# DeltaNet recurrence of a two-layer hybrid trunk: one projection step per recurrence step, split by tokens

## The reference, cut to what matters

```python
def step(state, inp):                      # scan over 8 chunks of 64 tokens, 8 heads, 64 x 64 states
    q_i, k_i, u_i, w_i, a_i, g_i = inp
    v_new = u_i - einsum('bhck,bhkv->bhcv', w_i, state)
    o = (einsum('bhck,bhkv->bhcv', q_i * exp(g_i)[..., None], state)
         + einsum('bhcs,bhsv->bhcv', a_i, v_new))
    g_last = g_i[..., -1]
    state = (state * exp(g_last)[..., None, None]
             + einsum('bhck,bhcv->bhkv', k_i * exp(g_last[..., None] - g_i)[..., None], v_new))
    return state, o
...
proj = h @ w_in[l]                         # a_v is 512 columns of this product
y_a = spatial_gating_branch(a_u, a_v, ...)
```

## Time and profile before

| what | us |
|---|---|
| median of 3 runs | 1763.38 (1763.12 to 1763.38) |
| the profiled execution | 1764.11 |
| its span on the core | 1762.3 |
| PE busy | 1744.1 (99%) |
| PE weight loads busy | 1426.3 (81%) |
| VectorE busy | 958.8 (54%) |
| POOL busy | 1066.3 (61%) |
| ScalarE busy | 689.9 (39%) |

### The profile page before, as it was taken

One profiled execution on the slowest core, in us unless ns is written; L12 is line 12 of the kernel. 1 busy time (PEld: TensorE's weight loads), 2 busy tenths in 40 slices (PEclk: granted clock), 3 DMA queues, 4 the chain that ended last, 5 costly groups with the idle time before them and its releaser, 6 DMA issues.

```text
span 1762.3 us, 26300 instructions
## 1 busy us (share of the span) xinstructions
PE 1744.1 (99%) x10006; PEld 1426.3 (81%) x10006; DVE 958.8 (54%) x1565; ACT 689.9 (39%) x1241; POOL 1066.3 (61%) x572
## 2 busy tenths in 40 slices
PE   8999999999999999999999999999999999999999
PEld 7778888778888888888787788887788888888887
DVE  6786636653542455444576866266443435444445
ACT  6433316650104444444355243075411054444442
POOL 6444367235665777777774434662456657777776
PEclk9999999999999999999999999999999999999999
DMA  6222133123235666666542222331332356666655
GB/s 201 85 69 77 49 96 108 37 96 96 84 97 169 157 172 161 161 174 157 130 156 78 71 70 61 96 96 37 108 96 85 97 158 163 159 173 158 169 154 144
DMA packets 58897, 207.18 MB, mean 118 GB/s; under 512 B 6369, under 2 KB 8705, under 8 KB 58785
## 3 DMA queue, kind: packets, MB, share of 16 engines
q1 hardware_dynamic: 47520, 164.94, 29.9%
q0 software_dynamic: 9216, 33.56, 10.2%
q10 hardware_dynamic: 2048, 7.10, 1.1%
HBM read 184.61 MB, written 4.19 MB: 107 GB/s over the span
## 4 chain that ended last, share of the span: by engine, by line
PE 95%; ACT 2%; DVE 2%; issue 1%; DMA 0%; SPq 0%; DVEq 0%; ACTq 0%
PE ps L662 22%; PE ps L664 22%; PE ps L663 22%; PE ps L1259 6%; PE ps L1261 6%; PE ps L1260 6%; PE ps L1131 2%; PE ps L1140 1%; PE ps L1153 1%; PE ps L681 1%; PE ps L904 1%; PE ps L891 0%; DMA xin<-x 0%; PE ps L941 0%; PE ps L1203 0%
## 5 line engine op out<-in xcount | busy, mean ns | idle before, releaser
L662 PE MATMUL ps<-hHi,wHi 128*128 128x512 f32 x1360 | 553.2, 407 | 1.3 <-DVE convd L1916 1.3
L664 PE MATMUL ps<-hHi,wLo 128*128 128x512 f32 x1360 | 530.4, 390 | 0.0
L663 PE MATMUL ps<-hLo,wHi 128*128 128x512 f32 x1360 | 529.8, 390 | 0.0
L562 POOL TENSOR_SCALAR wHi<-wraw 128x1024 fp32r<-128x1024 f32 x168 | 181.4, 1080 | 497.3 <-PE ps L664 480.2
L567 POOL TENSOR_TENSOR wLo<-wraw,wHi 128x1024 fp32r<-128x1024 f32 x168 | 415.2, 2472 | 13.9
L593 POOL TENSOR_TENSOR wLo<-w,wHi 128x1024 fp32r<-128x1024 f32 x96 | 239.2, 2514 | 138.6 <-ACT wHi L1690 138.0
L662 PEld LDWEIGHTS ps<-hHi,wHi 128*128 128x128 f32 x1360 | 255.4, 188 | 61.5 <-issue 6.9
L663 PEld LDWEIGHTS ps<-hLo,wHi 128*128 128x128 f32 x1360 | 255.7, 188 | 54.7 <-issue 3.8
L664 PEld LDWEIGHTS ps<-hHi,wLo 128*128 128x128 f32 x1360 | 255.3, 188 | 54.2
L1259 PE MATMUL ps<-wHi,fHi 128*128 128x512 f32 x448 | 174.8, 390 | 1.8 <-issue 1.8
L1260 PE MATMUL ps<-wLo,fHi 128*128 128x512 f32 x448 | 174.3, 389 | 0.0
(11 more groups left out here) (334 smaller groups left out, 2675.0 us busy)
## 6 DMA issues: line engine op xcount, KB each, us to landing
wraw<-stream SPq DMA_DIRECT2D x224, 512.0 KB, 3.6
w<-stream SPq DMA_DIRECT2D x64, 512.0 KB, 4.4
w<-w POOLq DMA_DIRECT2D x32, 512.0 KB, 6.9
b<-stream SPq DMA_DIRECT2D x16, 512.0 KB, 3.5
b<-stream POOLq DMA_DIRECT2D x16, 512.0 KB, 6.4
w<-stream POOLq DMA_DIRECT2D x16, 512.0 KB, 8.1
xin<-x SPq DMA_DIRECT2D x4, 512.0 KB, 6.8
y<-x ACTq DMA_DIRECT2D x1, 2048.0 KB, 9.9
```

The source lines that it names most:

```text
L562: nc.gpsimd.tensor_scalar(wHi[:, slot], wraw[:, slot % RAW], 1.0, 0.0, ALU.mult, ALU.add).then_inc(unit_high, 1)
L662: mm(o, lh[lc], rh[rc], start=start, stop=False)
L663: mm(o, lh[lc], rl[rc], start=False, stop=False)
L664: return mm(o, ll[lc], rh[rc], start=False, stop=stop)
```

## The change

The block of the projection is cut by tokens. `project_half(tile, k, 0)` does the three products on tokens 0 to 255 and stands where the whole block stood. `project_half(tile, k, 1)` does them on tokens 256 to 511 and stands after the queries of line 916, ahead of the wait for `vnew`. Six matmuls of 128x256 take the place of three of 128x512 in each of the steps 0 to 7. Both halves write one bank; only the first matmul of the first half opens the sum.

```diff
+                def project_half(tile, k, half):
+
+                    n, u = TILE_NO[tile], UNIT_NO[tile]
+                    if k == 0 and half == 0:
+                        pe.wait_ge(bank_read[n % 2], layer * per.bank_read + n // 2)
+                        pe.wait_ge(unit_split, layer * per.unit_split + u + 1)
+                    o = tile_bank(layer, n)[:, half * 256:(half + 1) * 256]
+                    weights, tokens = np.s_[:, u % RING, k * P:(k + 1) * P], np.s_[:, k, half * 256:(half + 1) * 256]
+                    mm(o, wHi[weights], hHi[tokens], start=k == 0 and half == 0, stop=False, skip_group_check=True)
+                    mm(o, wHi[weights], hLo[tokens], start=False, stop=False, skip_group_check=True)
+                    last = mm(o, wLo[weights], hHi[tokens], start=False, stop=k == KD - 1, skip_group_check=True)
+                    if k == KD - 1 and half:
+                        last.then_inc(unit_done, 1)
+
...
                         if step < CHUNKS:
-                            project(("av", 1), range(step, step + 1))
+                            project_half(("av", 1), step, 0)
                         else:
                             turn_delta_output(0)
...
                     if step == 0:
-                        project(("av", 1), range(0, 1))
+                        project_half(("av", 1), 0, 0)
...
                     if step:
                         last.then_inc(query_done, 1)
+                    if step < CHUNKS:
+                        project_half(("av", 1), step, 1)
                     for half in range(2):
                         pe.wait_ge(vnew_done, layer * per.vnew_done + 2 * step + half + 1)
```

## The result

| | median us | lowest to highest |
|---|---|---|
| before | 1763.38 | 1763.12 to 1764.77 |
| after | 1773.30 | 1772.60 to 1773.81 |

The ratio is 1.0054, with a 95% interval of 1.0038 to 1.0070: slower by 9.9 us, where 8.9 were forecast. The profiled execution took 1773.27 us against 1764.11, its span 1771.4 against 1762.3, so +9.1.

What follows compares the result with a forecast made beforehand. PE was taken to bound the kernel, busy 99% and 95% of the chain. Steps 1 to 7 add 4.43 us per layer, twice 8.9, moving the median 1763.38 to 1772.3; range 1770.5 to 1774.5, 8 in 10 1768.0 to 1776.0.

Steps and rivals of the forecast that it cites:

- The first place gives nothing back in steps 2 to 7: Ahead of line 904: block 0.32 us shorter, but line 904's second half still waits for r; gain at most 0.02, counted 0.
- The second half block is paid in full: Between lines 916 and 927, where no wait hides it: +0.72 us in even steps, +0.67 in odd ones.
- the change of tile size: Between 64x64 and full-size matmuls: 0.20 us going in against 0.05, 0.10 coming out; without this drain +5.4 instead of +8.9.
- Step 1: Recurrence step 1: r doesn't hold line 904, so 0.32 us is gained before the added half block; net +0.34, bounds 0.3 and 0.65.
- Step 6: Recurrence step 6: VectorE also scales an output chunk; its 0.08 us extra goes with line 927 later, leaving +0.64.
- Step 0: Recurrence step 0: both half blocks in succession, line 927 possible at 168.26 but waiting for vnew until 168.36; counted 0.
- Seven steps, two layers: Sum over steps 1 to 7: 4.43 us per layer, twice is 8.9.
- A: Rival: PE's own order holds line 904's second half, so steps 2 to 7 gain 0.32 us each; 1768.5, chance 0.08.
- B: Rival: short streams don't hide their weight loads, so a 128x256 matmul costs 0.23 us; +15.3, 1778.7, chance 0.07.
- C: Rival: at least 0.7 us idle ahead of line 927 holds the half block; seven steps lose 0.32 each, 1758.9, chance 0.04.
- D: Rival: PE waits behind the recurrence, for weights or POOL, shorten; between 0 and +3.5 us, say 1765, chance 0.04.
- Both it and PE move by the same amount, so its distance to PE stays: POOL's ring refill after the tile is done: POOL already waits 21.0 us, so the later tile adds no term.

## Why the prediction was right, and where it was not

- *The first place gives nothing back in steps 2 to 7.* Right: the second half of the `gated` times r products starts 1.75 us into the step in the changed kernel and in the variants with half a block or nothing in the first place and the full r. The wait named, the second half of r, is the one: a faster r sets PE free.
- *The second half block is paid in full.* Right: +0.70 measured in steps 2 and 4 against 0.72, +0.62 to 0.63 in odd ones against 0.67. Of the small excess 0.02 is the half block itself: 0.55 from its first load to the next, not 0.57. The price put on the change of tile size also holds: 0.15 going in, 0.11 for the first load and 0.10 coming out make 0.36, and 64x64 products in its place saved 0.34 in step 2.
- *Step 1.* 3.44 against 3.16: +0.28 for 0.34 forecast. *Step 6:* its 0.08 went, as said (3.98, like the other even steps): +0.61 for 0.64. *Step 0:* nothing, as said: line 943's wait for vnew is still there.
- *Seven steps, two layers.* 8.3 measured, 8.9 forecast.
- *Rivals.* A, B and C are out by the rows above. D too: the two terms found sum to 9.3, the spans differ by 9.1, so a later wait took up 0.2 at most.
- *"Both it and PE move by the same amount, so its distance to PE stays"*, the step on POOL. This failed. POOL, released by the tile's last matmul, starts its refill 1.4 us later within step 7 (3.24 into it, before 1.81), while the step itself grew by only 0.6; so `wLo` begins 0.7 later against step 8, on top of the scaling of `o_tm`. It cost 0.96, of which the prediction had nothing. The two errors, 0.6 too much and 1.0 missing, nearly cancel: that the total of the profiled pair, 9.1, lies so near the 8.9 is in part luck.
- *The medians.* They differ by 9.9 and the profiled pair by 9.2; the interval of the ratio, 6.7 to 12.3 us, holds both.

## What to carry to other kernels

A wait that is already filled to its end can't be filled better by cutting the filler: look which half of the awaited thing comes last, and compare that moment, not the start of the wait, with the end of the filler. A second visit to a wait pays the fixed price of the visit again, here 0.35 us for going from 64x64 tiles to the full array and back, and an apparent wait has to be longer than that before it is worth filling. When work moves, the signals at its end move with it; follow each one to the engine that it starts, and look what that engine then lies on top of.

## What the runs showed of the hardware

- A VectorE instruction with two SBUF inputs, the scaling of `o_tm`, took 0.69 us alone and 1.50, 2.22 or 2.47 beside a POOL instruction of 2.35, and ended 0.54 to 0.55 after it.
- 128x256 fp32r matmuls start 0.12 us apart, with new weights each; into a block of full size it is 0.20 from the last 64x64 load (0.05 between two groups of 64x64), the first load is open for 0.11, and 0.10 is lost on the way out.
- Less work took longer: with one half block less in each step, PE stood idle more, and three of four runs had a mean granted clock of 0.998 to 0.996 and took 1774.3 to 1778.4 us, where the fourth, at 1.00, took 1772.1. In the profiled one the granted clock stood at 1.2 instead of 2.4 GHz for 6.8 us in each layer. In the four runs where only steps 2 to 7 were thinned out it stayed at 1.00.
